# Scaling projected tokens in place before plain transposes, ahead of an up projection, and squares taken two pieces later

## The reference, cut to what matters

```python
m = jnp.concatenate([a, p], axis=-1) @ w_o[l]
x = x + rms_norm_2(m, post_mix_g[l])
h = rms_norm_2(x, pre_ffn_g[l])
up = causal_dwconv(h @ w_up[l], conv_w[l], conv_b[l])
y = (gelu(up[..., :D_FF_2]) * up[..., D_FF_2:]) @ w_down[l]
```

## Time and profile before

| | us |
|---|---|
| median of 3 runs | 2149.03 |
| lowest, highest | 2148.25, 2149.92 |
| the profiled execution | 2148.78 |
| its span in the trace | 2147.0 |
| TensorE busy | 2128.6 (99%) |
| VectorE busy | 1286.2 (60%) |
| ScalarE busy | 1064.4 (50%) |
| GpSimd busy | 242.2 (11%) |

### The profile page before, as it was taken

The page is one execution under the profiler, slowest core; times in us unless marked ns, Lnnn a source line. Parts: engine busy times, 40 slices in busy tenths (PEclk is TensorE's granted clock), DMA queues, the critical chain, the costliest instruction groups (busy, mean ns, idle before and its releaser), DMA issues.

```text
span 2147.0 us, 28153 instructions
## 1 busy us (share of the span) xinstructions
PE 2128.6 (99%) x11698; PEld 1848.7 (86%) x11698; DVE 1286.2 (60%) x1335; ACT 1064.4 (50%) x1198; POOL 242.2 (11%) x135
## 2 busy tenths in 40 slices
PE   8999999999999999999999999999999999999998
PEld 7888888888888888888888888888888888888886
DVE  6555556655555565565669655576666644566655
ACT  6554554545334443444554544455455433554553
POOL 3000001100000000000224000032222100222211
PEclk9999999999999999999999999999999999999999
DMA  8555555565656655665566555545665666566563
GB/s 279 162 174 174 177 166 187 177 205 167 211 191 183 196 185 192 177 205 189 191 193 193 178 175 181 182 148 179 193 196 177 215 193 189 167 187 202 191 199 113
DMA packets 207472, 399.50 MB, mean 186 GB/s; under 512 B 12400, under 2 KB 15600, under 8 KB 207088
## 3 DMA queue, kind: packets, MB, share of 16 engines
q1 hardware_dynamic: 207056, 395.60, 58.4%
q10 hardware_dynamic: 288, 2.10, 0.3%
HBM read 395.55 MB, written 2.10 MB: 185 GB/s over the span
## 4 chain that ended last, share of the span: by engine, by line
PE 98%; DVE 1%; ACT 0%; DMA 0%; issue 0%; SPq 0%; DVEq 0%; ACTq 0%
PE ps L1336 98%; DMA raw<-in_sb_w_qkv_dram 0%; PE ps L1339 0%; DVE raw L1234 0%; DVE Wl L1024 0%; DVE E L1063 0%; ACT E L862 0%; ACT E L860 0%; ACT T L958 0%; ACT zs L855 0%; DVE QK L1213 0%; ACT E L858 0%; ACT L860 0%; ACT Wh L812 0%; DVE aHL L1186 0%
## 5 line engine op out<-in xcount | busy, mean ns | idle before, releaser
L1024 DVE TENSOR_TENSOR Wl<-raw,Wh 128x1024 fp32r<-128x1024 f32 x745 | 920.4, 1256 | 618.0 <-ACT Wh L812 617.1
L1336 PE MATMUL ps<-aHL,Wh 128*128 128x512 f32 x3328 | 1164.4, 395 | 8.3 <-DVE Wl L1020 6.5
L812 ACT ACTIVATE Wh<-raw 128x1024 fp32r<-128x1024 f32 x745 | 768.6, 1054 | 608.3 <-PE ps L1336 602.9
L1336 PE MATMUL ps<-aHL,Wl 128*128 128x256 f32 x3328 | 931.9, 280 | 0.0
L1336 PEld LDWEIGHTS ps<-aHL,Wh 128*128 128x128 f32 x3328 | 624.7, 188 | 150.7 <-DVE aHL L1014 6.5
L1336 PEld LDWEIGHTS ps<-aHL,Wl 128*128 128x128 f32 x3328 | 629.7, 189 | 0.4
L1336 PE MATMUL ps<-hid,Wh 128*128 128x512 f32 x1024 | 355.1, 391 | 0.0
L1336 PE MATMUL ps<-hid,Wl 128*128 128x256 f32 x1024 | 286.9, 280 | 0.0
L1336 PEld LDWEIGHTS ps<-hid,Wh 128*128 128x128 f32 x1024 | 191.5, 187 | 41.9
L1336 PE MATMUL ps<-Wh,hid 128*128 128x512 f32 x704 | 217.6, 390 | 0.0
L1336 PEld LDWEIGHTS ps<-hid,Wl 128*128 128x128 f32 x1024 | 193.8, 189 | 0.0
(11 more groups left out here) (171 smaller groups left out, 1290.4 us busy)
## 6 DMA issues: line engine op xcount, KB each, us to landing
raw<-in_mlp_w_dram SPq DMA_DIRECT2D x256, 512.0 KB, 4.3
raw<-in_w_up_dram SPq DMA_DIRECT2D x176, 512.0 KB, 3.9
raw<-in_sb_w_qkv_dram SPq DMA_DIRECT2D x95, 512.0 KB, 4.8
raw<-in_w_down_dram SPq DMA_DIRECT2D x88, 512.0 KB, 4.2
raw<-in_w_in_dram SPq DMA_DIRECT2D x64, 512.0 KB, 4.4
raw<-in_sb_w_o_dram SPq DMA_DIRECT2D x32, 512.0 KB, 4.4
raw<-in_w_o_dram SPq DMA_DIRECT2D x32, 512.0 KB, 4.0
xT<-in_x_dram SPq DMA_DIRECT2D x8, 256.0 KB, 7.9
```

Source lines behind the costliest of these rows:

```text
L812: e.activation(Wh[:, i % NW, :], rawv[:, i % NRAW, :], ACT.Copy).then_inc(st["hi"][0], 1)
L1024: e.tensor_tensor(Wl[:, i % NW, :], rawv[:, i % NRAW, :], Wh[:, i % NW, :].bitcast(F32), ALU.subtract).then_inc(st["lo"][0], 1)
L1336: return e.matmul(o, l, r, start=start, stop=stop, skip_group_check=True)
```

## The change

D and its product are gone. Instead `xn` is multiplied by r in place, strip by strip (four strips n of 512 features, two halves t of 128 tokens), and TensorE transposes the scaled blocks by the identity. Strips 0 and 1 are scaled straight behind r: half 0 on VectorE, half 1 on ScalarE. Then VectorE copies the kept strip, and the first group follows. Both halves of strip 2 are scaled on ScalarE behind group 1 (before the split of U5), both of strip 3 on ScalarE behind U1. The `squares` steps are registered four pieces behind their group and no longer two.

```diff
-            r, diag = done("rms_r"), done("rms_diag")
+            r = done("rms_r")
...
+            scaled = {}
+
+            def scale_rows(n):
+                scaled[n] = [done("row_scaled_dve" if n < 2 else "row_scaled_act"), done("row_scaled_act")]
+                step("scale_rows", n=n, r=r, kept=kept[1] if n == 3 else None, done=scaled[n])
...
-                step("mixed_tiles", j0=j0, b0=b0, set=s, need=[diag, *bank_free[b0 // 2]], turns=turns, groups=groups)
+                step("mixed_tiles", j0=j0, b0=b0, set=s, need=[*scaled[j0 // 4], ident, *bank_free[b0 // 2]], turns=turns, groups=groups)
...
-                free[f"set{s}"], free["zs"] = [res], [turns[1]]
-                later(2, lambda: squares(j0 // 4, ("xT", j0 // 4), [res]))
+                free[f"set{s}"] = [res]
+                later(4, lambda: squares(j0 // 4, ("xT", j0 // 4), [res]))
+            scale_rows(0)
+            scale_rows(1)
+            step("keep_last", set=s, kept=kept)
             tiles(0)
+            scale_rows(2)
+            later(1, lambda: scale_rows(3))
             for n in (1, 2, 3):
                 later(n, lambda n=n: tiles(4 * n))
...
+                elif k == "scale_rows":
+                    cs = slice(st["n"] * STRIP, (st["n"] + 1) * STRIP)
+                    e.wait_ge(*st["r"])
+                    if st["kept"]:
+                        e.wait_ge(*st["kept"])
+                    for t in (1,) if st["n"] < 2 else (0, 1):
+                        e.activation(xn[:, t, cs], xn[:, t, cs], ACT.Copy, scale=cols["a"][:, t:t + 1]).then_inc(st["done"][t][0], 1)
...
-                    for t in st["zs_free"]:
-                        e.wait_ge(*t)
-                    diagonal(cols["a"], st["r"], st)
+                elif k == "scale_rows" and st["n"] < 2:
+                    cs = slice(st["n"] * STRIP, (st["n"] + 1) * STRIP)
+                    e.wait_ge(*st["r"])
+                    e.tensor_scalar(xn[:, 0, cs], xn[:, 0, cs], cols["a"][:, 0:1], None, ALU.mult).then_inc(st["done"][0][0], 1)
+                elif k == "keep_last":
                     e.tensor_copy(xn[:, 1, 3 * STRIP:4 * STRIP], ps[st["set"]][:, 1, :]).then_inc(st["kept"][1][0], 1)
...
-                                m = mm(P[:, b0 + n, a * 256 + t * 128:a * 256 + (t + 1) * 128], xn[:, t, j * 128:(j + 1) * 128],
-                                       D[:, t * 128:(t + 1) * 128], True, True)
+                                m = tp(P[:, b0 + n, a * 256 + t * 128:a * 256 + (t + 1) * 128], xn[:, t, j * 128:(j + 1) * 128])
```

More of the change, by code:

```diff
@@ L420, in f @@
             rec, sq2, prod = done("rms_rec"), done("rms_rec"), done("rms_rec")
-            r, diag = done("rms_r"), done("rms_diag")
+            r = done("rms_r")
             step("mixed_norm", set=s, sq=sq, kept=kept, warm=warm, total=total, mean=mean, root=root, rec=rec, sq2=sq2,
-                 prod=prod, r=r, diag=diag, ident=ident, zs_free=list(free["zs"]))
+                 prod=prod, r=r)
+            scaled = {}
+            def scale_rows(n):
+                scaled[n] = [done("row_scaled_dve" if n < 2 else "row_scaled_act"), done("row_scaled_act")]
+                step("scale_rows", n=n, r=r, kept=kept[1] if n == 3 else None, done=scaled[n])
             bank_free = [list(kept), []]
```

## The result

The changed kernel takes 2151.05 us (median of 22 runs, 2149.96 to 2157.36), the kernel before 2149.31 in the same rounds (22 runs, 2148.13 to 2153.22). The ratio is 1.0016 with a 95% interval of 1.0009 to 1.0022: slower by less than 0.2%, so no change by the bound set ahead, and slower by its own interval. The profiled execution took 2150.87 us, its span is 2149.1, 2.1 longer than before.

The account below looks back on a forecast made before the run. TensorE was taken as the bound, the norm's diagonal leading it by only 0.43 us. Later GpSimd sums delay that diagonal, +1.9 us, hiding TensorE's saving: 2150.7 us profiled, 2150.9 median, range 2146.8 to 2153.6.

Parts of the forecast that it names:

- Group of transposes: TensorE: eight transposes take 0.82 us instead of 1.70 for products, 0.88 saved a group; three groups count, 2.6 us.
- First addition: VectorE, first scaled tile: the addition starts at 1392.80 instead of 1392.92, 0.1 us gained.
- Groups 2, 3, 4: VectorE/ScalarE ping-pong: group 2 starts at 1399.48 (was 1399.11), rounds take 5.41 us, group 4 starts at 1410.30 (was 1410.40).
- GpSimd: Sums of all four squares: 10.9 us undisturbed plus 3.7 for four disturbances, ending at 1430.15, 2.1 us later than before.
- Sum to diagonal: VectorE: strip's addition starts 0.11 us after the last GpSimd sum; from it to the diagonal's end 6.18 us, giving 1436.44.
- Spread: TensorE's product that wants the new norm's diagonal: starts at 1436.69 instead of 1434.77.
- TensorE's waits: Two new waits: some 2.7 us behind U11 for the strip's addition, some 2 us behind U12 for the diagonal.
- A: Rival: the products' saving comes through and TensorE is never late, -2.7 us, 2146.3; with near cases, chance 0.18.
- B: Rival: ping-pong stays at 5.88 us and GpSimd is disturbed as densely as before, +3.8 to +5.5 us; chance 0.15.
- C: Rival: transposes drop TensorE's clock to 1.2 GHz over U1, 3 to 4 us, absorbed by a later wait: +1.9 to +2.5; chance 0.05.
- D: Rival: transposes bring TensorE nothing, same time as the main forecast since it waits anyway; chance 0.62 together with that forecast.
- The sum of +1.9 us: Whole change: TensorE's product with the diagonal moves from 1434.77 to 1436.69, so the kernel is 1.9 us slower.

Follow-up runs that it names:

- kernel 10: Changed kernel with all four squares in free buffers, two pieces behind their group, the second group's square only one behind: 2146.68 us, ratio 0.9989.
- kernel 6: Changed kernel with the column sums on TensorE moved behind U12, so its two waits become one: 2154.34 us, ratio 1.0023.
- kernel 4: Changed kernel with squares 2 and 4 in an unread part of QK instead of T1, squares two pieces behind: 2147.99 us, ratio 1.0000.
- 1: Changed kernel with the squares two pieces behind their group again, as before: 2149.68 us, ratio 1.0004.
- 3: Changed kernel with squares 2 and 4 in an unread part of QK instead of T1, squares four pieces behind: 2151.61 us, ratio 1.0015.
- 7: Changed kernel with each group's eight transposes done as plain products with the identity: 2151.23 us, ratio 1.0013.
- 2: Kernel before with only the squares moved, to four pieces behind their group: 2151.43 us, ratio 1.0014.
- 5: Changed kernel with TensorE filling its wait behind U11 with 14 products of ones with zeros: 2151.57 us, ratio 1.0014.
- 8: Changed kernel with all four squares in free buffers, two pieces behind their group: 2147.58 us, ratio 0.9988; again 2147.72, ratio 0.9991.
- 9: Kernel before with its squares in free buffers, two pieces behind their group: 2148.55 us, ratio 0.9997.

## Why the prediction was right

Counted from the root, as predicted and as measured:

- *Group of transposes:* 0.82 us; 1398.92 - 1398.13 = 0.79.
- *First addition:* 2.78 behind the root; 2.51. The scaling in place takes 0.48 us, between the bounds 0.43 and 0.68, where I took the upper; so VectorE decided, as said, but 0.3 us sooner. The Trainium skill ("VectorE: DVE Perf Modes", § Mode 2×_2P) has such an operation at double rate; the row agrees more with that than with the 0.69 of the copy, which reads PSUM.
- *Groups 2, 3, 4:* 9.46, 14.87, 20.28; 9.14, 14.54, 19.95. The two ScalarE scalings delay group 2 as worked out and each round of the ping-pong lasts 5.4 us.
- *GpSimd:* begins at 25.54, lasts 14.59; 25.30 and 1430.39 - 1415.82 = 14.57. Disturbed steps are those beside the splits, four as counted: 1.61 for 0.8, 2.28 for 1.30, 1.63 for 0.74, 1.80 for 0.73.
- *Sum to diagonal:* 0.11 + 6.18 us; 1430.50 - 1430.39 = 0.11 and 1436.68 - 1430.50 = 6.18.
- *Spread:* 46.67; 46.22. The 0.45 us too much are the 0.3 of the first addition (0.24 of it left at GpSimd's start) and 0.2 of TensorE's start, for which I had 0.25 and which took 0.06.
- *TensorE's waits:* 2.7 us behind U11; 3.2, since U1 began 4.71 us behind the root and not 4.98, and U5 to U11 ran at the quicker pair pitch here (last section). Behind U12 2 us were expected; there the clock fell, which the prediction did not foresee, U12 took 1436.74 - 1432.31 = 4.4 us, and only a rest of the wait was left.

Of the rivals, A (the saving comes through) is what kernel 10 does and the changed kernel doesn't. B (5.88 a round, denser disturbance) didn't happen. C happened in another place: TensorE was busy for 1.63 us only in 1391.80 to 1395.20 and the clock stayed at 1.00, so the Trainium skill's rule on transposes ("TensorE: Matmul & The Clock Gate", § Part 4: PE-mode transpose) showed no effect of its own here; it was the wait behind U11 that lowered it. That the wait for the diagonal takes the cost, as C had it, held only because the fall lay ahead of it, and that was luck: kernel 6 shows it uncovered. C also counts 4.6 us behind U12, which by the prediction's own working are both waits together, 2.7 of them ahead of U12. D (the transposes bring nothing) is right but for the 0.5 us of the first group. The sum of +1.9 us is +1.5 in the stretch and +2.1 in the span. The median of the runs is 2151.05 us, 2150.9 was foreseen. That this is so close is in part luck: the kernel before took 2149.31 in these rounds and not 2149.03, and the median holds the upper group, of which the prediction knew nothing; in the lower group the difference is +1.3.

## What to carry to other kernels

An engine that is 99% busy is not the bound at every place: before shortening its work, look how far ahead of it the next operand is (here 0.43 us), and follow that operand's chain back through every queue and buffer. Choose the place of a background job on a slow engine (GpSimd) by when its last result is wanted, not only by the load of the engine that feeds it: two pieces later on ScalarE was 1.8 us later at the diagonal (46.16 us behind the root, 44.32 before). Give such a job buffers that the main line doesn't write.

## What the runs showed of the hardware

**Two pitches of TensorE at the same clock.** A pair of products of the up projection (128x512 by the high part, 128x256 by the low part) starts every 0.346 to 0.347 us in one execution and every 0.353 to 0.354 in another, for a whole run of strips, at a granted clock of 1.00 in both. Kernel before, then kernel 4, at the same place, every second pair:

```profile
1500.03 0.39 PE L1336 MATMUL ps<-aHL,Wh 128*128 128x512 f32 x1
...
1500.72 0.39 PE L1336 MATMUL ps<-aHL,Wh 128*128 128x512 f32 x1
...
1501.42 0.39 PE L1336 MATMUL ps<-aHL,Wh 128*128 128x512 f32 x1
```

```profile
1500.07 0.40 PE L1355 MATMUL ps<-aHL,Wh 128*128 128x512 f32 x1
...
1500.77 0.40 PE L1355 MATMUL ps<-aHL,Wh 128*128 128x512 f32 x1
...
1501.48 0.40 PE L1355 MATMUL ps<-aHL,Wh 128*128 128x512 f32 x1
```

Behind U13 the profiled executions of kernels 1, 3, 4 and 7 had the slower pitch and the other nine the quicker one, and these four are those whose time lies in the upper group. From the spread to the end of the span they took 716.8 to 717.0 us, the others 712.2 to 712.4 (kernel 6, where the clock cost 2.0, 714.4). So this is the upper group of runs, as far as thirteen traces show it. It held 31 of 87 runs of the kernels in which TensorE is held up by the diagonal (the changed kernel and 1, 2, 4 to 7), 2 of 55 of those in which it isn't (3, 8 twice, 9, 10), and 14 of 115 of the kernel before. But that wait is not what sets the pitch by itself. Kernel 3 has the slower pitch without it. Kernels 1, 4 and 7 had it in U9 to U11 already, ahead of the wait, and so had the kernel before (pairs at 1424.83, 1425.18, 1425.53 and 1425.89), which went on at the quicker one behind U12 without any wait there. What sets the pitch stays open.

**The clock after a wait.** After 3.2 us without work (changed kernel) the clock was at its 1.2 GHz level for 3.4 us, from some 1.6 us behind the restart (shares of 0.85 and 0.81 in two windows of 5 us are 1.5 and 1.9 us at half); after 3.5 us (kernel 3: 0.74 and 0.58) for 6.8, which cost 2.9 us; with the wait of 4.3 us (kernel 6: 0.96, 0.50 and 0.86) also for 6.8, of which some 2.4 lay in the wait. With the wait of 1.8 us before U1, with only transposes ahead of it, it stayed at the 2.4 GHz level.
